# Moving the start addresses of weight slots, stage input, constants and stage tiles in a matmul-dominated fp32 transformer kernel

## What is computed

```python
def swiglu_ffn(h, w_in, w_out):
    gate, up = jnp.split(h @ w_in, 2, axis=-1)
    return (jax.nn.silu(gate) * up) @ w_out

def sq_relu_mlp(x, w1, w2):
    return jnp.square(jax.nn.relu(x @ w1)) @ w2
```

## The kernel before, in words

| tiles | before | after the change |
|---|---|---|
| `w_raw`, `w_hi_part`, `w_lo_part` (slots 0 to 4) | 128 | 0 |
| `wx_raw`, `wx_hi_part`, `wx_lo_part` (slots 5 to 7) | 448 | 0 |
| `x_res`, `xn` | 128 | 0 |
| `h_hi_part`, `h_lo_part`, `const`, `cols` | 128 | 64 |
| `row` | 416 | 64 |
| `stats` | 480 | 128 |
| stage tiles of the feed-forward, ple, gla, mla and conv stages (`hid_hi_part`, `ple_hi_part`, `mc_hi_part`, ...) | 480 | 64 |
| the first part's mixer: `conv_hi_part`, `conv_lo_part`, `glu`, `hc`, `gdn_w` | 384 | 64 |

## Time and profile before

### The profile page before, as it was taken

How to read it: one execution, slowest core, us unless ns; L and a number is a source line. 1 busy time by engine, 2 the same in 40 slices (tenths; PEclk the granted TensorE clock), 3 DMA queues, 4 the chain that set the end, 5 groups by cost and what they waited for, 6 DMA issues and landing times.

```text
span 3032.2 us, 38314 instructions
## 1 busy us (share of the span) xinstructions
PE 2904.8 (96%) x15292; PEld 2440.4 (80%) x15292; DVE 1934.0 (64%) x2858; ACT 1538.0 (51%) x2235; POOL 74.8 (2%) x99
## 2 busy tenths in 40 slices
PE   8999998899999999988999999999999999999999
PEld 6879987678878799876788878877887878787887
DVE  5556977575565569875755675465645754567545
ACT  5544744355555447443554545545545445554554
POOL 0000000000000000000000000000000000000000
PEclk9999999899999999998999999999999999999999
DMA  7544510255555445102555535543555555453552
GB/s 285 183 132 161 171 50 22 104 182 192 183 180 187 133 160 174 49 22 104 175 200 184 173 105 199 184 163 122 205 181 184 185 183 181 159 191 104 185 184 80
DMA packets 127809, 470.03 MB, mean 155 GB/s; under 512 B 14494, under 2 KB 14654, under 8 KB 126480
## 3 DMA queue, kind: packets, MB, share of 16 engines
q1 hardware_dynamic: 124560, 453.08, 43.9%
q0 software_dynamic: 3072, 14.51, 1.4%
HBM read 466.48 MB, written 1.05 MB: 154 GB/s over the span
## 4 chain that ended last, share of the span: by engine, by line
PE 80%; DVE 13%; ACT 4%; issue 2%; POOL 1%; DMA 0%; POOLq 0%; ACTq 0%; DVEq 0%
PE ps L585 77%; DVE w_lo_part L1961 3%; DVE hc L2268 2%; PE ps L762 2%; DVE conv_acc L2193 1%; PE ps L622 1%; ACT w_hi_part L1416 1%; DVE wx_lo_part L1961 0%; DVE h_lo_part L2004 0%; ACT wx_hi_part L1416 0%; DVE zs L2411 0%; POOL gdn_gate L2757 0%; ACT gdn_rhs L1691 0%; DVE x_res L2163 0%; DVE x_res L2105 0%
## 5 line engine op out<-in xcount | busy, mean ns | idle before, releaser
L1961 DVE TENSOR_TENSOR w_lo_part<-w_raw,w_hi_part 128x1024 fp32r<-128x1024 f32 x459 | 552.7, 1216 | 353.2 <-ACT w_hi_part L1416 351.8
L1416 ACT ACTIVATE w_hi_part<-w_raw 128x1024 fp32r<-128x1024 f32 x459 | 477.6, 1054 | 405.8 <-PE ps L585 405.8
L585 PE MATMUL ps<-w_hi_part,h_hi_part 128*128 128x512 f32 (+1 forms) x1348 | 543.1, 403 | 30.1 <-DVE w_lo_part L1958 7.4
L585 PE MATMUL ps<-w_hi_part,h_lo_part 128*128 128x512 f32 (+1 forms) x1348 | 529.0, 392 | 0.0
L585 PE MATMUL ps<-w_lo_part,h_hi_part 128*128 128x512 f32 (+1 forms) x1348 | 528.4, 392 | 0.0
L1961 DVE TENSOR_TENSOR wx_lo_part<-wx_raw,wx_hi_part 128x1024 fp32r<-128x1024 f32 x222 | 268.1, 1218 | 207.4 <-ACT wx_hi_part L1416 206.0
L1416 ACT ACTIVATE wx_hi_part<-wx_raw 128x1024 fp32r<-128x1024 f32 x222 | 231.7, 1055 | 232.1 <-PE ps L585 232.1
L585 PEld LDWEIGHTS ps<-w_hi_part,h_hi_part 128*128 128x128 f32 x1348 | 258.4, 192 | 90.3 <-issue 17.3
L585 PEld LDWEIGHTS ps<-w_hi_part,h_lo_part 128*128 128x128 f32 x1348 | 257.6, 191 | 55.9
L585 PEld LDWEIGHTS ps<-w_lo_part,h_hi_part 128*128 128x128 f32 x1348 | 258.6, 192 | 49.2
L585 PE MATMUL ps<-wx_hi_part,h_hi_part 128*128 128x512 f32 x684 | 273.6, 400 | 6.4 <-ACT lv L1754 2.1
(11 more groups left out here) (437 smaller groups left out, 4899.0 us busy)
## 6 DMA issues: line engine op xcount, KB each, us to landing
w_raw<-in_weights SPq DMA_DIRECT2D x569, 512.0 KB, 3.3
wx_raw<-in_weights SPq DMA_DIRECT2D x288, 512.0 KB, 3.4
row<-in_rows POOLq DMA_DIRECT2D x8, 1024.0 KB, 5.1
row<-in_rows POOLq DMA_DIRECT2D x8, 512.0 KB, 4.0
const<-in_const SPq DMA_DIRECT2D x1, 1088.0 KB, 15.9
x_res<-in_x SPq DMA_DIRECT2D x2, 512.0 KB, 6.5
ple_p<-in_p POOLq DMA_DIRECT2D x4, 256.0 KB, 4.9
out<-x_res SPq DMA_DIRECT2D x2, 512.0 KB, 2.6
```

Source lines behind the costliest of these rows:

```text
L585: return nc.tensor.matmul(out, lhsT, rhs_, start=start, stop=stop, skip_group_check=True)
L1416: A(hi_of(s)[:, 0:wd], raw_of(s)[:, 0:wd], ACT.Copy).then_inc(*up("w_hi", u))
L1961: V.tensor_tensor(lo_of(s)[:, 0:wd], raw_of(s)[:, 0:wd], hi[:, 0:wd], ALU.subtract).then_inc(*up("w_lo", u))
```

## The change

It adds tiles that nothing uses (gaps), widens two, moves the place of two in the list of tiles, and moves the memory in which slots 5 to 7 and the stage tiles lie. `NS_IN` and the three loops over units stay as they are; no line that issues an instruction is touched. `W_TOP` is the end of slots 5 to 7, `W_BASE` the start of the stage tiles; the two serve only for the size of `below` (line 480).

```diff
-W_BASE, W_TOP = 128512, 229344
+W_BASE, W_TOP = 129088, 228864
...
+        sb("first_gap", [P, 96])
         w_raw = sb("w_raw", [P, NS_IN, UW])
         w_hi = sb("w_hi_part", [P, NS_IN, UW], F32R)
         w_lo = sb("w_lo_part", [P, NS_IN, UW], F32R)
         x = sb("x_res", [P, NT, D])
         xn = sb("xn", [P, NT, D])
+        sb("h_gap", [P, 16])
         h_hi = sb("h_hi_part", [P, KC, SEQ], F32R)
         h_lo = sb("h_lo_part", [P, KC, SEQ], F32R)
         const = sb("const", [P, N_CONST, P])
         cols = sb("cols", [P, COLS.n])
+        sb("cols_gap", [P, 56])
         row = sb("row", [P, 2, 2, D])
         neghalf = sb("neghalf", [P, 16])
         st = sb("stats", [P, 4, 32])
+        sb("stats_gap", [P, 112])
...
         gate = sb("gdn_gate", [P, 12, 40], F32, m1)
+        lnm = sb("conv_ln", [P, 32], F32, m1)
         gnw = sb("gdn_norm", [P, 1, GDK], F32, m1)
-        lnm = sb("conv_ln", [P, 8], F32, m1)
         mw = ExitStack()
         glu = sb("glu", [P, KC, CONVB - 1 + SEQ], F32, mw)
+        sb("glu_gap", [P, 16], F32, mw)
...
-        sb("glu_end", [P, 256], F32, m1)
+        sb("glu_end", [P, 384], F32, m1)
...
         mkr = sb("mkr", [P, SEQ], F32, mw3)
+        mnorm = sb("mla_norm", [P, 1, 512], F32, mw3)
         mw3.close()
...
         rope = sb("rope", [P, SEQ], F32, m3)
-        mnorm = sb("mla_norm", [P, 1, 512], F32, m3)
...
         cpad = sb("cpad", [P, KC, 2 + SEQ], F32, m4)
+        sb("cpad_gap", [P, 112], F32, m4)
```

## The result

The changed kernel takes 3057.81 us (median of four runs, 3057.1 to 3060.32), the kernel before beside it 3036.11 us. The ratio is 1.0073, with a 95% interval of 1.0056 to 1.0091: 21.7 us slower, where 19.6 us faster had been forecast.

What follows compares the result with a forecast made beforehand. TensorE bounds most of the span: matmul count times start-to-start interval. Gains of 15.1 + 3.5 + 0 + 4.4 = 23.0 us, 0.85 let through, give 19.6 us and a median of 3017 us; range 2989 to 3046.

Steps and rivals of the forecast that it cites:

- Step 3: Input `h` from 128 to 64, slots 0 to 4 from 128 to 0, 3948 matmuls of 512 columns: no change.
- Step 2: Slots 5 to 7 from 448 to 0, 2052 matmuls over `h` fall from 229.4 to 227.7 ns: 3.5 us gained.
- Step 1: Hidden tile's two parts from 480 to 64, their 512-column matmuls fall to 227.7 ns: 15.1 us gained.
- Step 4: 256-column form, slots 0 to 4 from 128 to 0: 120.0 to 117.8 ns, 4.4 us gained; slots 5 to 7 nothing.
- rival A: All matmuls fall to 226.6 or 113.3 ns as streams no longer meet: 43.7 us gained, about 2995; chance 0.15.
- rival C: All 512-column matmuls go to 232.8 ns, stationary and moving starts 64 bytes apart: 25 us slower, 3062; chance 0.18.
- Step 5: VectorE's remainder and the PSUM splits on VectorE and ScalarE: the address does nothing to their times, 0 us.
- The operands left out of the count: The convolution, ple and mla operands, under 400 matmuls, left out of the counts.
- The share let through: Part of the 23.0 us sum expected to be seen at the end: 0.85, giving 19.6 us.

Runs made afterwards that it cites:

- stages_alone: The kernel before with only the stage tiles moved, from 480 to 128: 3026.09 us, ratio 0.9971 to the kernel before.
- mix_shift: all0, but the first part's two mixers write and read the stage input 64 bytes lower, in tiles 64 bytes longer: 3011.26 us, ratio 0.9917 to the kernel before.
- apart256: The changed kernel with stage input and stage tiles at 256, weight slots at 0: 3017.99 us, ratio 0.9933 to the kernel before.
- all0: The changed kernel with stage input, constants and stage tiles at 0 instead of 64, weight slots staying at 0: 3017.48 us, ratio 0.9941 to the kernel before.

## Why the prediction was wrong

**What bounds the kernel.** Right. Instructions and the other engines' work stayed, waits changed by a few us, and counts times intervals give +21.8 us where +21.7 was measured, the agreement in the last digit being luck.

**Step 3 failed**, and with it the forecast: "I take no change: both stay multiples of 64". The 3948 matmuls went from 228.4 to 233.3 ns, 19.3 us. What had been compared were tiles that each started somewhere; what decides is the distance, and step 3 took the pair from distance 0 to 64, which the 512-column form had nowhere before.

**Step 2** failed with it. Slots 5 to 7 over the input went from distance 192 to 64 and lost 7.2 us instead of gaining 3.5. With everything at 0 or at 64, where the distance is 0, that pair did fall, to 227.3 and 227.4 ns.

**Step 1** expected the hidden tile at 227.7 ns because 64 is a multiple of 64. It went to 233.4. In stages_alone, which moves it to distance 0 from slots 0 to 4, it came to 227.9: the level was right, the rule behind it wrong. "The only start that is no multiple of 64" was a coincidence of two distances, 96 and 32, both of them slow.

**Step 4** took 117.8 ns, and 117.7 came, 4.4 us as forecast. The number came by luck: what moved the level was the distance, from 0 to -64, and not the slots' start. Rows 12 against rows 10 had been read as no effect of the streamed tile: distances 160 and 0 happen to give 119.9 and 120.0. The same reading was then held against the distance in rival A, which lowered the chance of everything that hangs on a distance, rival C's included.

**Step 5** held: VectorE's remainder takes 1222 ns before and after, the splits of the input and the hidden values 684 and 682 ns. The operands left out of the count were 456 matmuls and not under 400; it changes nothing that matters.

**The share let through**, 0.85, could not be tested by the changed kernel, where no gain came. For everything at 0 the levels give -2.8 - 5.1 - 11.1 - 6.4 + 0.2 + 1.5 = -23.7 us, and -17.1 was measured, 0.72 of it. The traces show where the rest went. Between the two profiled executions the difference is 15.8 us; TensorE's idle time before the input's matmuls grew from 36.5 to 42.0 us, and 133 us were spent at the lower level of the clock against 126, which by the estimate above costs some 3 us. In the changed kernel the idle time grew too, but the clock gave back as much, so nearly the whole sum of the levels was seen.

**Rival C** is what happened, by its own mechanism ("the new pair may meet where the pair 128/128 does not") and nearly at its price: 232.8 ns were put into it and 233.3 to 233.4 came, 3062 us against 3057.8. Its argument, the level of rows 9, was the right one to follow: of all stretches it had starts nearest to each other. It was given 0.18, and the range ended at its half, 3046. Of rival A this much is true, that the lowest level of each form exists: 226.9 with everything at 0, 113.3 in the mixers of mix_shift; no single placement gives both.

**The rule of the Trainium skill** weighed in the prediction, that TensorE's two read ports are independent and wait for nobody (page "SBUF — State Buffer", section "Who interferes with whom"), does not hold here in the form in which the prediction used it, that every start is as good as another: two kernels with the same instructions, 64 bytes apart in one gap, differ by 40 us, and TensorE's intervals differ between them by more than that (21.8 + 23.7 = 45.5 us by levels). Whether the two ports wait for each other, or something behind them does, no run shows.

## What to carry to other kernels

For back-to-back float32r matmuls compare tiles in pairs: take stationary start minus streamed start modulo 256 and read the interval for each distance that occurs, before moving anything. With 512 streamed columns a distance of 0 was the best by 2 to 7 ns of 230, with 256 columns it was, beside +160, the worst by up to 6.7 ns of 120; put tiles of the first form on equal starts modulo 256, and try for the second form a view of the streamed tile 64 bytes lower where it dominates. A regularity in single addresses that rests on five or six pairs may be one of distances: look for two pairs that share the address and not the distance.

## What was not expected of the hardware

The start-to-start interval of equal matmuls takes between 226.9 and 234.0 ns in the 512-column form and between 113.3 and 120.0 ns in the 256-column form, depending for the most part on the difference of two start addresses. It repeats every 256 bytes (apart256 and all0 agree to 0.1 ns), depends on the sign (+64: 233.3, -64: 229.3), and goes with the matmul's own stationary tile, with an effect of the matmul ahead where the pair changes.
